# Half blocks of filler cut in two parts between scores and transposes, and the products of narrow attentions moved to VectorE ahead of the next maximum

## The chip, the cores and the metric

The kernel runs on one core of one Trainium2 chip. The metric is the time of one execution on the device, in microseconds; three runs of the kernel before gave 3421.99, 3423.82 and 3425.35 us, so the median is 3423.82 us. The profile is one more execution, recorded by the hardware profiler.

## The reference, cut to what matters

One sequence of 1024 tokens with 1024 features goes through three layers and two outer norms. All weights and activations are float32; the kernel splits each operand of a large product into a high and a low part and adds three products.

```python
# first_block, two layers: x = x + concat([mixed, mo]) @ w_out[l]; x = x + squared_relu_mlp(...)
#   layer 0: mixed = window_gqa (16 heads, 3 blocks of 128 keys, sink); layer 1: mixed = gated LRU
#   in both: mo = memory_attention(mq, mk, mv)
def memory_attention(mq, mk, mv):                      # 4 heads of 128, 256 memory tokens
    sc = einsum('bshd,bmhd->bhsm', mq, mk) * MEM_HEAD_DIM ** -0.5
    return einsum('bhsm,bmhd->bshd', softmax(sc, -1), mv)

# second_block, one layer on the output of the first, after its final norm
proj = h @ w_in                                        # h: modulated norm, 1024 x 3328
sb_q, sb_k, sb_v, sb_g, sw_q, sw_k, sw_v, sw_g = split(proj)
y_sb = stick_breaking_attention(sb_q, sb_k, sb_v) * silu(sb_g)      # 8 heads of 64
#   z = q k / 8; w = exp(log_sigmoid(z) + sum of log_sigmoid(-z) over the later keys), s < t
y_sw = sliding_window_sink_attention(sw_q, sw_k, sw_v) * silu(sw_g) # 8 heads, 256 keys, sink
x = x + gate * (concat([y_sb, y_sw]) @ w_out)
return rmsnorm(x, final_g)
```

## The kernel before, in words

Activations lie transposed, features on partitions and tokens on columns. A weight block is 128 x 1024: eight pieces of 128 x 128. `piece` and `split` (lines 228 to 249) load a block, copy it to its high part on ScalarE and subtract for the low part on VectorE, two blocks ahead of use; the load of a block three further on is issued on SP. A product of one block with 512 tokens is a "half chunk" (`half_chunk`, lines 351 to 371): 8 pieces x 3 = 24 matmuls of 512 columns into one PSUM bank, and a function `leave` that evacuates the bank. Half chunks are the filler of three kinds of stage.

All instructions are put in five queues in the order of the program text (class `Queues`, lines 40 to 111); each engine runs its own queue in order, and waits on the semaphores of an instruction's dependencies. So the order of calls is the schedule.

**Attention with units** (`attention_units`, lines 463 to 573). A unit is four heads (or, in the memory attentions, four blocks of queries) of 128 queries. It is used four times: with 384 keys ("full", 32 units of two groups of two, layer 0's window attention) and, narrow, with up to 256 keys, one group of four: the two memory attentions (8 units each) and the sliding-window attention of the last layer (16 units; units 0 and 1 have 128 keys). In step u the calls come in this order: `scores(u)`: matmuls on TensorE, the maximum of each row on VectorE (line 491), the negated maximum, with a sink also a sum for the sink, four exponentials on ScalarE with their sums, and the sink's exponential; `normalise(u-1)`: sum, reciprocal, and four products of a row's probabilities with its reciprocal, two on VectorE (line 515, recorded as line 148) and two on POOL (line 517); if `fills[u]` is 2, one filler call; `values(u-2)`: matmuls with V, and in every second unit the output block; the unit's side work if it has any; `turn(u-1)`: eight transposes on TensorE (line 526), which wait for the products; `copies(u-1)`: one bank copied by ScalarE, one by VectorE (line 539); and, if `fills[u]` is 1 or 2, one filler call.

In the memory attentions filler is the output projection (`half_chunks`), each call a whole half chunk with its evacuation. In the sliding-window attention filler is the gate's projection (`gate_chunk`, lines 1421 to 1426): eight half chunks in one bank, 7; each call first evacuates the half chunk before it (tanh on ScalarE, a product on VectorE). Two come before unit 0, the others in units 0, 1, 3, 5, 7 and 9. Output blocks (`out2`, line 1439) are a product on VectorE, a high copy on ScalarE and a subtraction on VectorE. Units 10 to 13 have side work: a row of 1024 columns is split into high and low (`to_parts`).

**Stick-breaking loop** (lines 1369 to 1405). 48 steps, each one block of 128 keys against up to 512 queries of two heads, pipelined over three steps. TensorE's order in step s is `pe_carry(s-3)`, `pe_within(s-2)`, `pe_scores(s)`, `pe_values(s-3)`, and in even steps up to 42 one half chunk (22 in all, in banks 6 and 7 in turn: gate, keys, queries). `pe_within` multiplies the high and the low part of a step's log terms, `sh` and `sl`, with a triangle. Behind TensorE's calls come those of ScalarE and VectorE: exponential, logarithm and combination `m` of step s-1, the copy of the scores of step s, the sum `add` of step s-2, `min` of step s, then `sh` on ScalarE and `sl` on VectorE of step s-1, and the last exponential of step s-2. A half chunk is evacuated at the end of the step behind it; a gate's evacuation is a tanh, with a table load before and one after it.

Of the kernel before, what the change touches and what calls it, by code (L numbers as in the profile page):

```python
# [13 lines left out]
KB = 1024  # L14
# [99 lines left out]
def program(nc, D, out, stop=None, dbg=None):  # L114
    ctx = ExitStack()
    with ctx:
# [234 lines left out]
        def half_chunk(name, bank, rhs, evac, hf, done):  # L351

            b = at[0]
            assert at[1] == 0
            piece(name)
            cs = slice(512 * hf, 512 * hf + 512)
            ps = PS[:, bank, :]
            for k in range(8):
                w = wsp[:, b % NS, :, k * 128:k * 128 + 128]
                rh, rl, ops = rhs(k)  # L360
                for i, (wi, r) in enumerate(((0, rh), (0, rl), (1, rh))):
                    op = mm(ps, w[:, wi, :], r[:, cs], k == 0 and i == 0, k == 7 and i == 2, splits[b], ops,
                            free[bank] if k == 0 and i == 0 else None)
            if done:
                uses[b] = [op]
                at[0] = b + 1

            def leave():
                free[bank] = [evac(cs, ps, op)]

            return op, leave

        def half_chunks(name, bank, rhs, evac):
            return [lambda n=n, hf=hf: half_chunk(name, bank, rhs, lambda cs, ps, op: evac(n, cs, ps, op), hf, hf == 1)[1]()
                    for n in range(8) for hf in range(2)]
# [87 lines left out]
        def attention_units(units, nkmax, off, scale, sink=None, fill=None, fills=()):  # L463
# [42 lines left out]
            def normalise(x):  # L506
                u, j, nk, sm_, es, rc, a = x
                if sink is not None:
                    a = TT(sm_, sm_, es, ALU.add, a)
                o = dve(lambda e: e.reciprocal(rc, sm_), a)  # L510
                last = [None, None]
                for i, pos in enumerate(groups[j]):
                    P_, r = Pb[:, u % 2, pos, 0:nk], rc[:, i:i + 1]
                    if i < w // 2:
                        last[0] = TS(P_, P_, r, None, ALU.mult, None, o)
                    else:
                        last[1] = pool(lambda e, P_=P_, r=r: e.tensor_scalar(P_, P_, r, None, ALU.mult), o)  # L517
                probs[J * u + j] = last
# [35 lines left out]
            for u in range(n + 2):  # L554
                for j in range(J):
                    x = scores(u, j) if u < n else None
# [3 lines left out]
                    if fill and fills[u] > 1:  # L560
                        fill.pop(0)()
# [8 lines left out]
                    if fill and fills[u] > 0:  # L570
                        fill.pop(0)()
# [734 lines left out]
        work = [lambda i=i, f=f, hf=hf: half_chunk("in2", 6 + i % 2, Hk, f(), hf, hf == 1)[1]  # L1306
# [62 lines left out]
        leave = None  # L1369
        for s in range(n_s + 3):  # L1370
# [8 lines left out]
            leaving, leave = leave, work.pop(0)() if s % 2 == 0 and work else None  # L1379
# [25 lines left out]
        assert not work and not leave  # L1405
# [13 lines left out]
        chunk, leave = [], []  # L1419

        def gate_chunk(t, hf):
            if leave:
                leave.pop()()
            op, late = half_chunk("in2", 7, Hk, fill_gate(WG, t, wg_done[t]), hf, True)
            chunk.append(op)
            leave.append(late)

        work = [lambda t=t, hf=hf: gate_chunk(t, hf) for hf in range(2) for t in range(4)]
        for _ in range(2):
# [19 lines left out]
        for k in range(4):  # L1449
            units[10 + k]["side"] = lambda k=k: to_parts(lambda _: SQ[:, k, :], lambda _: Hk(k), 1, chunk[7])  # L1450
        attention_units(units, 256, 80 * KB, 0.125, True, [*work[:2], lambda: leave.pop()(), *work[2:], lambda: leave.pop()()],
                        [1, 1, 1, 1, 0, 1, 0, 1, 0, 1, 1] + [0] * 7)
# [168 lines left out]
```

How the kernel before makes its waits and increments, by code:

```python
            def run(eng):  # L93
                seen = {}
                for o in self.q[name]:
                    for d in o.deps:
                        if seen.get(d.sem.name, 0) < d.val:
                            eng.wait_ge(d.sem, d.val)
                            seen[d.sem.name] = d.val
                    if o.fn is None:
                        continue
                    ins = o.fn(eng)
                    if o.sem is not None:
                        ins.then_inc(o.sem, 1 if o.sem is self.sems.get(name) else 16)
```

## Time and profile before

| | |
|---|---|
| median of 3 runs | 3423.82 us |
| profiled execution, its own time | 3419.25 us |
| its span, first to last instruction | 3417.5 us |
| granted TensorE clock, mean | 0.970 of full speed |
| TensorE busy | 3147.2 us, 92% |
| VectorE busy | 1689.4 us, 49% |
| ScalarE busy | 1112.8 us, 33% |
| POOL busy | 191.6 us, 6% |

Engines in the rows: PE is TensorE's matmuls, PEld its weight loads, DVE is VectorE, ACT is ScalarE, POOL is GpSimd, SP issues DMAs. "L283" is line 283, the helper `mm`, so matmuls are told apart by their operands: `PS<-H,wsp` is filler, `PS<-p,triR` the triangle products of the loop, L526 the transposes. Line 138 is the helper of ScalarE, 141, 144, 148 and 149 are those of VectorE. A row of a timeline is start, duration, engine, line, operation, output<-inputs, count; in brackets is the idle time of the engine ahead of it and who ended it. The stages of interest are the first memory attention (about 500 to 625 us), the second (1694 to 1830), the stick-breaking loop (2777 to 3122) and the sliding-window attention (3136 to 3312).

### The profile page before, as it was taken

How to read it: one execution, taken by the hardware profiler on the slowest of the kernel's cores; microseconds unless marked ns; L12 is line 12 of the kernel's file. 1: busy time of each engine (PE TensorE's matmuls, PEld its weight loads, DVE VectorE, ACT ScalarE, POOL GpSimd, SP SyncE). 2: the span in 40 equal slices, each digit the busy share in tenths (PEclk: the TensorE clock that was granted, in tenths of full speed). 3: DMA queues.
4: the chain of work that ended last, by engine and by line, in shares of the span. 5: the costliest groups of instructions: out<-in, count | busy, mean ns of one | idle time of the engine just before them, and what ended most of it. 6: DMA issues, size and time to landing. Idle time of an engine off the chain costs nothing.

```text
span 3417.5 us, 34713 instructions
## 1 busy us (share of the span) xinstructions
PE 3147.2 (92%) x14280; PEld 2419.9 (71%) x14298; DVE 1689.4 (49%) x2088; ACT 1112.8 (33%) x1729; POOL 191.6 (6%) x162
## 2 busy tenths in 40 slices
PE   4999989999999999999799999999997998997678
PEld 4777557778888888777677788888875775554456
DVE  6544864444444433589644433333336435554455
ACT  4202652311111111388523211111115336664332
POOL 0001431000000000000010000000003100000110
PEclk9999999999999999999999999999998999998889
DMA  4211011122222211211201111111111310002012
GB/s 163 99 38 32 1 55 33 37 74 73 69 74 69 73 50 54 76 47 47 99 31 44 43 50 50 44 50 48 45 49 56 117 37 19 19 19 74 19 50 99
DMA packets 54015, 190.19 MB, mean 56 GB/s; under 512 B 5984, under 2 KB 6368, under 8 KB 53728
## 3 DMA queue, kind: packets, MB, share of 16 engines
q1 hardware_dynamic: 53856, 187.96, 16.7%
q8 instruction: 113, 1.85, 0.2%
q14 instruction: 46, 0.38, 0.0%
HBM read 172.20 MB, written 14.68 MB: 55 GB/s over the span
## 4 chain that ended last, share of the span: by engine, by line
PE 76%; DVE 11%; ACT 9%; issue 2%; POOL 1%; DMA 0%; SPq 0%; DVEq 0%; ACTq 0%; POOLq 0%
PE PS L283 74%; ACT p L138 7%; DVE p L141 4%; PE PS L526 2%; DVE p L144 2%; DVE sm L491 2%; POOL p L517 1%; ACT H L138 1%; DVE p L1100 1%; ACT wsp L138 1%; DVE wsp L141 1%; DVE p L539 0%; ACT L138 0%; DVE p L149 0%; DVE sm L144 0%
## 5 line engine op out<-in xcount | busy, mean ns | idle before, releaser
L283 PE MATMUL PS<-H,wsp 128*128 128x512 f32 x6864 | 1617.8, 396 | 48.6 <-POOL H L1198 21.1
L283 PEld LDWEIGHTS PS<-H,wsp 128*128 128x128 f32 x6864 | 1299.8, 190 | 354.7 <-issue 28.4
L283 PE MATMUL PS<-p,wsp 128*128 128x512 f32 (+1 forms) x3840 | 896.2, 394 | 42.0 <-DVE p L141 21.5
L283 PEld LDWEIGHTS PS<-p,wsp 128*128 128x128 f32 x3840 | 714.3, 190 | 219.7 <-ACT wsp L138 37.7
L138 ACT ACTIVATE p<-p 128x1024 f32<-128x1024 f32 (+7 forms) x426 | 359.9, 871 | 852.0 <-DVE p L144 689.1
L138 ACT ACTIVATE wsp<-raw 128x1024 fp32r<-128x1024 f32 (+1 forms) x266 | 275.6, 1039 | 774.8 <-PE PS L283 632.6
L141 DVE TENSOR_TENSOR p<-p,PS 128x1024 f32<-128x1024 f32 (+2 forms) x232 | 244.3, 1053 | 526.4 <-PE PS L283 526.4
L141 DVE TENSOR_TENSOR wsp<-raw,wsp 128x1024 fp32r<-128x1024 f32 (+1 forms) x266 | 322.5, 1215 | 144.2 <-ACT wsp L138 144.1
L141 DVE TENSOR_TENSOR p<-PS,p 128x1024 f32<-128x1024 f32 (+1 forms) x124 | 143.0, 1153 | 442.6 <-PE PS L283 417.2
L283 PE MATMUL PS<-p 128*64 128x256 f32 (+9 forms) x1432 | 296.9, 480 | 15.0 <-DMA p<-mk_dram 5.0
L141 DVE TENSOR_TENSOR p<-p 128x1024 fp32r<-128x1024 f32 (+5 forms) x235 | 232.3, 991 | 112.1 <-ACT p L138 109.7
L517 POOL TENSOR_SCALAR p<-p,sm 128x256 f32<-128x256 f32 (+2 forms) x128 | 150.4, 1180 | 2297.2 <-DVE sm L510 2297.2
L138 ACT ACTIVATE p<-PS,sm 128x256 f32<-128x256 f32 (+2 forms) x256 | 127.9, 508 | 310.3 <-DVE sm L144 175.5
L144 DVE SCALAR_TENSOR_TENSOR p<-p 128x1024 f32<-128x1024 f32 (+3 forms) x167 | 189.3, 1141 | 68.4 <-ACT p L138 65.9
L138 ACT ACTIVATE p<-PS 128x512 f32<-128x512 f32 (+4 forms) x198 | 121.0, 638 | 264.1 <-PE PS L283 237.8
L283 PEld LDWEIGHTS PS<-p 128*64 128x64 f32 (+2 forms) x1432 | 127.5, 173 | 98.6 <-issue 60.5
L526 PE MATMUL PS<-cf,p 128*128 128x128 f32 x600 | 96.8, 300 | 79.6 <-POOL p L517 66.6
L526 PEld LDWEIGHTS PS<-cf,p 128*128 128x128 f32 x600 | 71.7, 152 | 115.5 <-issue 59.1
L491 DVE TENSOR_REDUCE sm<-PS 128x2 f32<-128x768 f32 (+3 forms) x96 | 94.9, 988 | 98.7 <-PE PS L283 98.2
L283 PE MATMUL PS<-p,triR 128*128 128x512 f32 (+3 forms) x352 | 86.5, 367 | 36.0 <-ACT p L138 19.8
L283 PEld LDWEIGHTS PS<-p,triR 128*128 128x128 f32 x352 | 56.5, 192 | 69.5 <-DVE p L141 34.3
L283 PE MATMUL PS<-wsp,H 128*128 128x256 f32 (+2 forms) x576 | 88.8, 316 | 0.0
(70 smaller groups left out, 1157.6 us busy)
## 6 DMA issues: line engine op xcount, KB each, us to landing
raw<-in_in_dram SPq DMA_DIRECT2D x70, 512.0 KB, 3.6
raw<-in_dn_dram SPq DMA_DIRECT2D x68, 512.0 KB, 3.5
raw<-in_up_dram SPq DMA_DIRECT2D x64, 512.0 KB, 3.5
raw<-in_out_dram SPq DMA_DIRECT2D x40, 512.0 KB, 3.6
p<-in_ada_dram SPq DMA_DIRECT2D x24, 512.0 KB, 4.5
raw<-in_kv_dram SPq DMA_DIRECT2D x16, 512.0 KB, 4.0
p<-in_x_dram SPq DMA_DIRECT2D x16, 512.0 KB, 8.7
spill_dram<-p SPq DMA_DIRECT2D x16, 512.0 KB, 2.9
```

The source lines that it names most:

```text
L138: return act(lambda e: e.activation(o, i, f, **kw), *a)
L141: return dve(lambda e: e.tensor_tensor(o, x, y, op), *a)
L144: return dve(lambda e: e.scalar_tensor_tensor(out=o, in0=x, scalar=s, in1=y, op0=op0, op1=op1), *a)
L283: return pe(lambda e: e.matmul(o, l, r, start=start, stop=stop, **kw), *a)
L491: o = dve(lambda e: e.tensor_reduce(mx, S, AX.X, ALU.max), op, prev)
L517: last[1] = pool(lambda e, P_=P_, r=r: e.tensor_scalar(P_, P_, r, None, ALU.mult), o)
L526: o = pe(lambda e, t_out=t_out, t_in=t_in: e.transpose(t_out, t_in, ident), probs[J * u + j], free[b])
L1100: L[("h", d)] = dve(lambda e: e.tensor_tensor_scan(out=dst, data0=da, data1=du, initial=0.0, op0=ALU.mult, op1=ALU.add), u, L[("a", d)], y ...
```

## The change: what it does

1. A half chunk is now a function `part(k0, k1)` that multiplies pieces k0 to k1 - 1, and `leave`. A whole one is `part(0, 8)`.
2. Loop: even steps up to 42 call `part(0, 4)`, the odd step behind each calls `part(4, 8)`; the evacuation comes at the end of the step behind that one, so one step later than before.
3. Sliding-window attention: each half chunk is two filler calls, `first` (evacuate the one before, 12 matmuls) and the rest (12 matmuls). Filler calls now all come between `scores(u)` and `values(u-2)`, none behind the transposes: two each in units 0, 1 and 2 (in unit 2: an evacuation alone, then a `first`), one each in units 3 to 10 (in unit 10 the last evacuation alone). So units 4, 6 and 8 begin a half chunk and units 3, 5, 7 and 9 end one.
4. Every narrow attention: all four products are on VectorE, and `normalise(u-1)` is called ahead of `scores(u)`, so it stands in VectorE's queue before the maximum of unit u.

The wide attention keeps its order and its products on POOL.

```diff
         def half_chunk(name, bank, rhs, evac, hf, done):
...
+            last = []
+
+            def part(k0, k1):
+                b = at[0]
+                assert at[1] == 0
+                piece(name)
+                for k in range(k0, k1):
...
+                last[:] = [op]
+                if done and k1 == 8:
+                    uses[b] = [op]
+                    at[0] = b + 1
 
             def leave():
-                free[bank] = [evac(cs, ps, op)]
-
-            return op, leave
+                free[bank] = [evac(cs, ps, last[0])]
+                return last[0]
+
+            return part, leave
...
-        def attention_units(units, nkmax, off, scale, sink=None, fill=None, fills=()):
+        def attention_units(units, nkmax, off, scale, sink=None, fill=None, fills=(), early=False):
...
-                    if i < w // 2:
+                    if i < w // 2 or not full:
                         last[0] = TS(P_, P_, r, None, ALU.mult, None, o)
                     else:
                         last[1] = pool(lambda e, P_=P_, r=r: e.tensor_scalar(P_, P_, r, None, ALU.mult), o)
...
                 for j in range(J):
+                    if pending and not full:
+                        normalise(pending)
+                        pending = None
                     x = scores(u, j) if u < n else None
                     if pending:
                         normalise(pending)
                     pending = x
-                    if fill and fills[u] > 1:
+                    for _ in range(fills[u] if fill and early else int(bool(fill) and fills[u] > 1)):
                         fill.pop(0)()
...
-                    if fill and fills[u] > 0:
+                    if fill and not early and fills[u] > 0:
                         fill.pop(0)()
...
-            leaving, leave = leave, work.pop(0)() if s % 2 == 0 and work else None
+            leaving = leave
+            leave = None
+            if s % 2 == 0 and work:
+                part, after = work.pop(0)()
+                part(0, 4)
+            elif s % 2 == 1 and after:
+                part(4, 8)
+                leave, after = after, None
...
+        def first(t, hf):
             if leave:
                 leave.pop()()
-            op, late = half_chunk("in2", 7, Hk, fill_gate(WG, t, wg_done[t]), hf, True)
-            chunk.append(op)
-            leave.append(late)
-
-        work = [lambda t=t, hf=hf: gate_chunk(t, hf) for hf in range(2) for t in range(4)]
-        for _ in range(2):
+            part, late = half_chunk("in2", 7, Hk, fill_gate(WG, t, wg_done[t]), hf, True)
+            part(0, 4)
+            leave.append(lambda: chunk.append(late()))
+            return part
+
+        for hf in range(2):
+            for t in range(4):
+                box = []
+                work.append(lambda t=t, hf=hf, box=box: box.append(first(t, hf)))
+                work.append(lambda box=box: box[0](4, 8))
+        for _ in range(4):
             work.pop(0)()
...
-        attention_units(units, 256, 80 * KB, 0.125, True, [*work[:2], lambda: leave.pop()(), *work[2:], lambda: leave.pop()()],
-                        [1, 1, 1, 1, 0, 1, 0, 1, 0, 1, 1] + [0] * 7)
+        attention_units(units, 256, 80 * KB, 0.125, True, [*work[:4], lambda: leave.pop()(), *work[4:], lambda: leave.pop()()],
+                        [2, 2, 2] + [1] * 8 + [0] * 7, True)
```

## Rows read from the trace of the kernel before

**Rows 1.** Stretches: length, then busy us (instructions) by engine, PEclk, DMA share, GB/s.

```profile
2788.60:3079.20 290.60, 263.00 (x1186) 165.80 (x1198) 161.82 (x203) 191.45 (x240) 0.00 (x0) 0.98 0.06 19
3150.18:3185.89 35.71, 24.35 (x110) 17.65 (x112) 12.62 (x28) 10.86 (x35) 4.45 (x6) 0.81 0.10 30
3185.89:3257.99 72.10, 48.89 (x242) 33.79 (x244) 29.41 (x61) 21.71 (x69) 11.91 (x12) 0.83 0.07 22
3257.99:3306.00 48.01, 27.85 (x165) 17.11 (x165) 30.24 (x63) 21.58 (x68) 13.90 (x14) 0.83 0.00 1
```

**Rows 2.** Waits of TensorE, 2788.64 to 3073.43: total us, times, longest.

```profile
PE PS L283 <- ACT p L138: 16.6, 19, 1.3
PE PS L283 <- DVE p L141: 8.5, 18, 1.1
```

**Rows 3.** Timeline of the loop, two steps of full width.

```profile
2933.44 5.74 PE L283 MATMUL PS<-H,wsp 128*128 128x512 f32 x24
...
2935.63 1.22 DVE L141 TENSOR_TENSOR p<-p 128x1024 fp32r<-128x1024 f32 x1 [0.25 <-ACT p L138]
...
2939.02 2.02 PE L283 MATMUL PS<-p,triR 128*128 128x512 f32 x8
...
2945.23 0.73 PE L283 MATMUL PS<-p,triR 128*128 128x512 f32 x2 [1.00 <-ACT p L138]
...
2946.49 0.73 PE L283 MATMUL PS<-p,triR 128*128 128x512 f32 x2 [0.53 <-DVE p L141]
```

**Rows 4.** Waits of all engines, 3122 to 3312.

```profile
PE PS L526 <- POOL p L517: 48.3, 16, 3.7
...
PE PS L283 <- DVE p L144: 12.3, 7, 3.8
```

**Rows 5.** Timeline of the loop behind a gate's evacuation.

```profile
2906.83 0.68 DVE L141 TENSOR_TENSOR p<-p 128x512 fp32r<-128x512 f32 x1
...
2908.49 1.08 PE L283 MATMUL PS<-p,triR 128*128 128x128 f32 x8
```

**Rows 6.** Timeline of the sliding-window attention, unit 7, and the maximum of unit 6.

```profile
3211.96 1.23 DVE L491 TENSOR_REDUCE sm<-PS 128x4 f32<-128x1024 f32 x1 [9.13 <-PE PS L283]
...
3218.80 1.22 DVE L491 TENSOR_REDUCE sm<-PS 128x4 f32<-128x1024 f32 x1 [0.92 <-PE PS L283]
...
3220.34 0.15 DVE L141 TENSOR_TENSOR sm<-sm 128x4 f32<-128x4 f32 x1
...
3220.74 0.84 DVE L148 TENSOR_SCALAR p<-p,sm 128x256 f32<-128x256 f32 x2
3220.80 1.99 POOL L517 TENSOR_SCALAR p<-p,sm 128x256 f32<-128x256 f32 x2 [4.85 <-DVE sm L510]
...
3222.21 0.63 ACT L138 ACTIVATE H<-p 128x512 fp32r<-128x512 f32 x1
...
3222.93 1.06 PE L526 MATMUL PS<-cf,p 128*128 128x128 f32 x8 [3.15 <-POOL p L517]
```

**Rows 7.** VectorE's groups by form, 2777 to 3312: busy us, mean ns | idle.

```profile
L539 DVE COPY p<-PS 128x512 f32<-128x512 f32 x14 | 9.7, 691 | 18.6 <-PE PS L526 18.5
...
L141 DVE TENSOR_TENSOR H<-p,H 128x1024 fp32r<-128x1024 f32 x4 | 4.9, 1226 | 3.9 <-ACT H L138 3.9
...
L149 DVE TENSOR_SCALAR p<-p 128x256 f32<-128x256 f32 x8 | 2.3, 285 | 0.0
```

**Rows 8.** Timeline of the sliding-window attention, unit 0.

```profile
3137.08 0.69 DVE L491 TENSOR_REDUCE sm<-PS 128x4 f32<-128x512 f32 x1 [5.34 <-PE PS L283]
...
3140.87 8.30 PE L283 MATMUL PS<-H,wsp 128*128 128x512 f32 x24 [3.83 <-DVE p L144]
```

**Rows 9.** Waits in the first memory attention, 500 to 622.

```profile
PE PS L526 <- POOL p L517: 5.4, 3, 2.1
```

**Rows 10.** Timeline of the second memory attention, unit 2.

```profile
1722.32 0.68 DVE L141 TENSOR_TENSOR p<-p,PS 128x512 f32<-128x512 f32 x1
...
1724.60 5.73 PE L283 MATMUL PS<-H,wsp 128*128 128x512 f32 x24
```

More of the change, by code:

```diff
@@ L351, in half_chunk, with whole @@
         def half_chunk(name, bank, rhs, evac, hf, done):
-            b = at[0]
-            assert at[1] == 0
-            piece(name)
             cs = slice(512 * hf, 512 * hf + 512)
             ps = PS[:, bank, :]
[L358 to L366, printed above, removed]
+            last = []
[4 more added lines that the diff above has]
+                for k in range(k0, k1):
+                    w = wsp[:, b % NS, :, k * 128:k * 128 + 128]
+                    rh, rl, ops = rhs(k)
+                    for i, (wi, r) in enumerate(((0, rh), (0, rl), (1, rh))):
+                        op = mm(ps, w[:, wi, :], r[:, cs], k == 0 and i == 0, k == 7 and i == 2, splits[b], ops,
+                                free[bank] if k == 0 and i == 0 else None)
+                last[:] = [op]
+                if done and k1 == 8:
+                    uses[b] = [op]
+                    at[0] = b + 1
             def leave():
-                free[bank] = [evac(cs, ps, op)]
-            return op, leave
+                free[bank] = [evac(cs, ps, last[0])]
+                return last[0]
+            return part, leave
         def half_chunks(name, bank, rhs, evac):
-            return [lambda n=n, hf=hf: half_chunk(name, bank, rhs, lambda cs, ps, op: evac(n, cs, ps, op), hf, hf == 1)[1]()
-                    for n in range(8) for hf in range(2)]
+            def whole(n, hf):
+                part, leave = half_chunk(name, bank, rhs, lambda cs, ps, op: evac(n, cs, ps, op), hf, hf == 1)
+                part(0, 8)
+                leave()
+            return [lambda n=n, hf=hf: whole(n, hf) for n in range(8) for hf in range(2)]
         Hops = [None] * 8
@@ L1305, in program @@
                 lambda: fill_keys(3), gate(3), *(lambda t=t: fill_query(t) for t in (1, 2, 3))]
[L1306 removed]
+        work = [lambda i=i, f=f, hf=hf: half_chunk("in2", 6 + i % 2, Hk, f(), hf, hf == 1)
                 for i, (f, hf) in enumerate((f, hf) for f in work for hf in range(2))]
@@ L1367, in pe_values @@
                     sg_free[pr] = o
-        leave = None
+        leave = after = None
         for s in range(n_s + 3):
@@ L1404, in program @@
                 leaving()
-        assert not work and not leave
+        assert not work and not leave and not after
         for par in range(2):
@@ L1418, in program @@
         wg_done = [[None, None] for _ in range(4)]
-        chunk, leave = [], []
-        def gate_chunk(t, hf):
+        chunk, work, leave = [], [], []
+        def first(t, hf):
             if leave:
                 leave.pop()()
-            op, late = half_chunk("in2", 7, Hk, fill_gate(WG, t, wg_done[t]), hf, True)
-            chunk.append(op)
-            leave.append(late)
-        work = [lambda t=t, hf=hf: gate_chunk(t, hf) for hf in range(2) for t in range(4)]
-        for _ in range(2):
+            part, late = half_chunk("in2", 7, Hk, fill_gate(WG, t, wg_done[t]), hf, True)
[8 more added lines that the diff above has]
+        for _ in range(4):
             work.pop(0)()
```

## The prediction

> **What bounds it now.** I read the busy shares of the page first (the table above): TensorE is busy for nearly all of the span and no other engine for half of it, so only TensorE's gaps, and the stretches in which its clock is halved, can be won. The table of stretches then says where the gaps are. The stick-breaking loop with filler, 2788.6 to 3079.2, has 290.6 us with 263.0 busy. The sliding-window attention, here from the maximum of unit 1 to the last transposes, is busy only some two thirds of the time, at a mean clock of 0.81 to 0.83 of full speed [rows 1]. The change touches nothing else, but for the two memory attentions; the loop's last steps have no filler and stay as they are.
>
> In the loop, the waits of TensorE are 16.6 us for ScalarE and 8.5 us for VectorE [rows 2]. The timeline of one pair of steps shows which: after the step with 24 filler matmuls (5.74 us) nothing is waited for, since VectorE's low part was done at 2935.63 + 1.22 = 2936.85, over 3 us before its reader. In the step without filler, TensorE waits 1.00 us for ScalarE's high part and 0.53 us for VectorE's low part [rows 3]. All filler covers one step, none the other.
>
> In the window attention two waits stand out: 48.3 us ahead of the transposes for POOL's normalisation, and 12.3 us for the bank of a filler chunk [rows 4].
>
> **Loop.** Removed: 24 matmuls in one place; added: 12 and 12. No instruction is added. Half of 5.74 is 2.87 us of cover for each step. In the step that had none, the waits 1.00 + 0.53 are under 2.87, so they go. The step that loses 2.87 us had a margin: 2939.02 plus half of 2.02 (the carries) plus two within matmuls, about 2940.5, against 2936.85, so 3.6 us. The tight place is behind a gate evacuation: low part ready at 2906.83 + 0.68 = 2907.5, wanted at about 2909.2 [rows 5], margin 1.7, which would leave 1.2 us of stall; but the evacuation now comes a step later. ScalarE and VectorE were busy 191 and 162 of 290 us [rows 1], so they can follow a loop some 25 us shorter. Evacuations, splits of weights and their loads on SP keep their order; a part's bank is the other one of two, free two steps on. Of the 25.1 us of waits, bounds are all gone and 10 gone; I take 21, leaving 4 around the eight gate evacuations. The clock of 0.98 is half speed for 4% of 290 us, which costs 5.8 us; fewer gaps may give back 0 to 5.8, I take 2. Loop: **-23 us** (-31 to -10).
>
> **Window attention, one unit at full width.** Now: maximum from 3218.80, exponentials and the sink's own until ScalarE is free at 3222.21 (3.4 us), POOL's two products 3220.80 to 3222.79, transposes 3222.93, 4.13 us behind the maximum [rows 6]. The unit's period, from maximum to maximum, is that plus 1.06 of transposes and some 1.7 of scores, 3218.80 - 3211.96 = 6.84 us [rows 6].
>
> With the change VectorE does all four products and has them ahead of the next maximum. That makes a ring on VectorE: maximum, wait for the exponentials (3.48 us from the maximum's start, the sink's included), sum and reciprocal (0.40, from 3220.34 to the first product [rows 6]), four products. The price of a product: 0.42 us in its present place beside POOL (two in 0.84, [rows 6]); 0.285 us for the nearest row without POOL, another constant-operand product of 256 columns [rows 7]. POOL will be idle, so I take 0.285 and keep 0.42 for the range. The Trainium skill ("SBUF — State Buffer", Terms) says that VectorE and GpSimd arbitrate for one port pair and the loser blocks for the other's whole instruction. By it a product without POOL would be cheap, as taken; without it, the sum below would be 6 us worse. With this rule the trace does not quite agree: both engines' products are recorded side by side [rows 6].
>
> Ring of a plain unit: 3.48 + 0.40 + 1.14 = 5.02 us. With an output block (every second unit) come ScalarE's copy 0.63 [rows 6], the bank copy 0.69 [rows 7] and a subtraction of the same width, taken to be as long, in order ahead of the next normalisation: 6.96. Units 10 to 13 also split a query row (1.23 on VectorE [rows 7], and a copy on ScalarE ahead of it, taken as 1.05): 7.9 to 8.45.
>
> Filler steps now come ahead of the transposes, but a chunk's first part evacuates the chunk before it, behind the unit's exponentials. The row of unit 0 shows that stall: 3140.87, which is 3.8 us behind the maximum at 3137.08 [rows 8]; with 256 columns the maximum is 0.5 longer and the exponentials 0.4: 4.8 us. So a pair of units from 4 on: 4.8 stall, part 2.87, values 1.0, transposes 1.0, bank copy 0.7, normalisation 1.54 = 11.95 for the first; the second, whose output block has to wait for the values behind its part, ends its normalisation 7.65 later: 19.6 us at full clock. Three such pairs now take 72.10 us [rows 1], 24.0 each. Of these 2 x 6.84 + 5.74 + 1.4 = 20.8 is the chain at full clock (1.4: the 12.3 us of bank waits [rows 4] less unit 0's 3.8, over six waits), and some 3 the halved clock. The stall with scores in front is a TensorE gap of 6.5 us, longer than today's 3.15; I add 2 us a pair for half clock behind it: 3 x 21.6 = 64.8, so -7.3.
> - Unit 1 to the maximum of unit 2: stall 3.8, a chunk as long as unit 0's 8.3 [rows 8], transposes 0.6, scores 1.7 = 14.4; units 2 and 3, a pair without output block in its first values: 19.9. Together 34.3 for 35.71 [rows 1]: -1.4.
> - Units 10 to 14: 8.45 + 8.45 + 7.93 + 8.45 + 5.02 = 38.3, unit 15 up to its transposes 7.1: 45.4 for 48.01 [rows 1]: -2.6.
>
> Window: -7.3 - 1.4 - 2.6 = **-11.3 us** (-18 to +5).
>
> **Memory attentions.** They keep their filler behind the transposes; only the normalisation moves. The first has 5.4 us of waits for POOL in three units [rows 9]; normalising during the scores saves all of two and half of the third: **-4.8** (-5.4 to -2). In the second, VectorE's queue also holds side work. Two normalisations of 1.35 us (without the sink's sum) now stand in front of maxima that start later, so ScalarE's split and the evacuation at 1722.32 come some 2.6 us later, past 1724.60, where the next chunk begins [rows 10]: **+1** (-2 to +3). The wide attention keeps its order and its POOL half: 0.
>
> **Sum.** -23 - 11.3 - 4.8 + 1 = -38.1 us. The profiled execution took 3419.25 us, which gives 3381.1; it lies 4.6 us under the median 3423.82, so **3386 us**.
>
> **Rivals.**
> - *The window attention gives nothing.* The stall for the bank is the long TensorE gap, and part, values and transposes behind it all run at half clock: a pair is 19.6 + 4.7, and with products at 0.42 another 1.1: 25.4, three are 76.2, 4 us slower than now; units 10 to 15 then cost 6 x 0.54 - 2.6 = +0.6, units 1 to 3 nothing. Window +5, total -22: 3402. For: the mean clock is already 0.83 there. Against: it is granted by stretches that need not meet the part. The Trainium skill ("TensorE: Matmul & The Clock Gate", HAM oscillation) has this rule, short bursts between waits keep the clock low; the trace agrees with it. Chance 0.21.
> - *The loop wins half.* The gate's activation and its two table loads on ScalarE meet steps whose cover is halved; eight stalls of 1.2 to 1.5 us stay: loop -12, total -27: 3397. Chance 0.15.
> - *Waits only move* from the bare step to the other, and the window is even: -5 or less: 3420. Chance 0.06.
> - *Slower.* Filler in the covered step was all needed: every even step then stalls 2.87 us, 22 x 2.87 = 63, less 25 won, +38 in the loop; with -15 elsewhere +23: 3447. It decides where the margin behind the 5.74 us is under some 1.2 us. The rows show 3.6 and 1.7. Chance 0.04.
>
> **Numbers.** The forecast has 0.54, its own range 3370 to 3395. A measurement of this kernel tells about 0.2%, 7 us, from no change. Faster by more: 0.54 + 0.21 + 0.15 = 0.90; within: 0.06; slower: 0.04. The range goes from all lower bounds (-31 - 18 - 5.4 - 2 = -56, 3367) to 6 us above the first rival, 3408; outside are the last two cases and thin tails.
>
> **What would show it.** In the loop, TensorE's waits for ScalarE and VectorE under 8 us in all, filler in groups of 12, the stretch some 268 us long. In the window attention no wait for POOL, products near 0.29 us, a wait of some 5 us for VectorE ahead of every second part, normalisations directly in front of maxima, and pairs of 20 to 22 us. Products at 0.42 us, pairs over 24 us or loop waits still above 15 us would prove the corresponding step wrong; a loop longer than 290 us would overthrow the forecast.

## The result and the profile after

The changed kernel takes 3371.86 us (median of four executions, 3369.49 to 3372.85) against 3422.90 us for the kernel before (four executions, 3418.16 to 3425.35): a ratio of 0.9852, 95% interval 0.9834 to 0.9869. That is 51 us faster, where 38 were forecast, and inside the predicted range of 3367 to 3408 us. The profiled execution took 3372.85 us, its span is 3371.1 us, 46.4 less than before's 3417.5.

The table divides both spans at the same instructions. Idle is the length less TensorE's busy time; "half clock" is the time, in us, in which TensorE was granted the lower of its two clocks.

| stretch | before, us | after, us | difference | half clock, before and after |
|---|---|---|---|---|
| up to the first memory attention | 500.0 | 503.5 | +3.5 | |
| first memory attention | 132.6 | 125.5 | -7.1 | 3.4, 0 |
| second memory attention | 140.9 | 143.1 | +2.2 | 18.7, 18.5 |
| loop, first scores to the gate's filler | 346.0 | 311.5 | -34.5 | 23.9, 6.8 |
| filler ahead of the window's first maximum | 13.9 | 15.5 | +1.6 | 0, 3.4 |
| window, first maximum to output projection | 175.0 | 159.4 | -15.6 | 64.9, 65.7 |
| behind it | 105.3 | 108.2 | +2.9 | 8.2, 16.0 |

The rest, in which the program is the same, differs by under 1 us.

**The loop.** These are the stretches of the profile of after: the loop's steps with filler, its steps without, then in the window units 1 to 3, 4 to 9, and 10 to 15 as far as the last transposes. Columns as in [rows 1].

```profile
2776.47:3051.80 275.33, 269.25 (x1262) 171.76 (x1263) 164.92 (x211) 202.45 (x252) 0.00 (x0) 0.99 0.07 22
3051.80:3088.00 36.20, 25.16 (x92) 10.82 (x92) 22.66 (x22) 24.05 (x25) 0.00 (x0) 0.95 0.00 1
3116.19:3150.32 34.13, 24.00 (x108) 17.19 (x108) 13.74 (x34) 10.82 (x35) 0.00 (x0) 0.80 0.09 31
3150.32:3213.48 63.16, 45.55 (x248) 31.54 (x248) 30.85 (x73) 21.57 (x69) 0.00 (x0) 0.84 0.08 26
3213.48:3257.57 44.09, 31.01 (x156) 17.26 (x157) 30.61 (x72) 20.88 (x68) 0.00 (x0) 0.74 0.00 1
```

The same two parts of the loop in the kernel before:

```profile
2777.15:3079.20 302.05, 273.78 (x1229) 173.22 (x1244) 164.43 (x208) 197.54 (x248) 0.00 (x0) 0.98 0.06 20
3079.20:3123.18 43.98, 31.64 (x110) 13.19 (x111) 25.07 (x25) 26.91 (x28) 0.00 (x0) 0.88 0.00 1
```

The filler now reaches one step further, so the two rows are best added. Idle time: 346.0 - 305.4 = 40.6 before, 311.5 - 294.4 = 17.1 after, so 23.5 us less. Busy time: 305.4 before, 294.4 after, 11.0 us less for the same matmuls, and that is what the forecast had at 2. The trace of before lacks 16 of the loop's 1352 matmul records, so a little of its busy time is counted as idle. The kernels e2 and e3 below have the loop undivided and all 1352 records: 38.6 us idle, 306.2 us busy, 20.5 us at half clock. Against them the division takes away 21.5 us of idle time and 11.8 of busy time. Waits of TensorE in after, in the part with filler, in the form of [rows 2]:

```profile
PE PS L283 <- DVE p L141: 5.6, 9, 1.4
PE PS L283 <- DVE p L911: 2.7, 1, 2.7
```

Against [rows 2], ScalarE's waits are gone, and of VectorE's half are left by count and two thirds by length (the one of line 911 stands ahead of the loop's first step, in before too). Two steps of the widest kind in after, where every 12 matmuls of filler stand ahead of eight triangle products, none of which waits:

```profile
2925.37 2.02 PE L283 MATMUL PS<-p,triR 128*128 128x512 f32 x8
...
2928.97 3.02 PE L283 MATMUL PS<-H,wsp 128*128 128x512 f32 x12
...
2931.24 1.22 DVE L141 TENSOR_TENSOR p<-p 128x1024 fp32r<-128x1024 f32 x1
2931.82 2.02 PE L283 MATMUL PS<-p,triR 128*128 128x512 f32 x8
```

Eight triangle products take 2.02 us; in [rows 3] the last four of the bare step came two at a time, each pair with a wait ahead of it and 0.73 us long instead of 0.50. By these records, whose ends are modelled, a wait costs its length and about 0.2 us more. The other part of the 11 us is the clock: half clock fell from 23.9 to 6.8 us, and 17.1 us at the lower level are worth at most half, 8.5. How the 11 us divide between the two was not measured.

**The window attention.** TensorE's largest waits in after, from the last filler ahead of it to the output projection, against [rows 4]:

```profile
PE PS L283 <- DVE p L144: 31.1, 6, 6.2
PE PS L283 <- ACT p L138: 8.0, 6, 2.6
PE PS L534 <- DVE p L148: 3.7, 6, 0.8
```

POOL's 48.3 us are gone. The wait for the filler's bank (line 144 is the evacuation's product) has grown from 12.3 to 31.1 us, six times about 5 us instead of seven times about 1.8. The timeline of after from the products of unit 7 to the maximum of unit 9, against [rows 6]:

```profile
3191.68 1.14 DVE L148 TENSOR_SCALAR p<-p,sm 128x256 f32<-128x256 f32 x4
3192.73 1.22 DVE L499 TENSOR_REDUCE sm<-PS 128x4 f32<-128x1024 f32 x1
...
3196.09 0.60 ACT L138 ACTIVATE p<-PS 128x512 f32<-128x512 f32 x1
...
3196.73 0.69 DVE L144 SCALAR_TENSOR_TENSOR p<-p,PS 128x512 f32<-128x512 f32 x1 [2.38 <-ACT p L138]
...
3197.47 4.48 PE L283 MATMUL PS<-H,wsp 128*128 128x512 f32 x12 [6.21 <-DVE p L144]
...
3205.36 3.01 PE L283 MATMUL PS<-H,wsp 128*128 128x512 f32 x12
3206.10 1.22 DVE L499 TENSOR_REDUCE sm<-PS 128x4 f32<-128x1024 f32 x1
```

The products stand directly ahead of the maximum, four in 1.14 us. The tanh of the evacuation (3196.09) comes behind the unit's four exponentials, so the bank is free 4.7 us behind the maximum of unit 8; TensorE has been idle for 6.2 us by then, and the first part runs partly at half clock, 4.48 us for what takes 3.01 in the second. A pair of units is 13.4 to 14.0 plus 7.4 us.

**The memory attentions.** TensorE's wait for the products in the first one, in after, against [rows 9]:

```profile
PE PS L534 <- DVE p L148: 0.3, 1, 0.3
```

Unit 2 of the second one, timeline of after, against [rows 10]:

```profile
1720.94 0.68 DVE L141 TENSOR_TENSOR p<-p,PS 128x512 f32<-128x512 f32 x1
...
1721.68 4.61 PE L283 MATMUL PS<-H,wsp 128*128 128x512 f32 x12 [3.35 <-DVE p L141]
```

The 5.4 us for POOL became 0.3. In the second, the chunk now waits 3.35 us for the bank that the evacuation at 1720.94 frees. The line counts only the 12 matmuls up to the end of the view, at 1726; the whole chunk of 24 took 7.37 us, with 3.4 us of it at half clock, against 5.73 in [rows 10].

### The profile page after: what moved, and what is told of

Same layout as the page of the kernel before. It is cut to its first block, busy times and chain, and to the rows that moved or that the text cites. A ratio compares the mean times of both kernels' runs of the same rounds, so it can differ in the third digit from the quotient of the medians.

```text
span 3371.1 us, 34684 instructions
## 1 busy us (share of the span) xinstructions
PE 3144.4 (93%) x14298; PEld 2421.0 (72%) x14298; DVE 1695.2 (50%) x2152; ACT 1113.1 (33%) x1729; POOL 128.8 (4%) x98
## 3 DMA queue, kind: packets, MB, share of 16 engines
q1 hardware_dynamic: 53856, 187.96, 17.1%
## 4 chain that ended last, share of the span: by engine, by line
PE 74%; DVE 12%; ACT 11%; issue 2%; POOL 1%; DMA 0%; SPq 0%; DVEq 0%; ACTq 0%; POOLq 0%
PE PS L283 73%; ACT p L138 8%; DVE p L141 4%; DVE p L144 2%; DVE sm L499 1%; PE PS L534 1%; ACT H L138 1%; ACT wsp L138 1%; DVE p L1111 1%; DVE p L148 1%; DVE H L141 1%; DVE wsp L141 1%; ACT L138 1%; DVE p L547 0%; DVE p L149 0%
## 5 line engine op out<-in xcount | busy, mean ns | idle before, releaser
L283 PE MATMUL PS<-p,wsp 128*128 128x512 f32 (+1 forms) x3840 | 897.3, 394 | 42.1 <-DVE p L141 21.6
L283 PE MATMUL PS<-p 128*64 128x256 f32 (+9 forms) x1432 | 290.7, 470 | 23.3 <-ACT p L138 10.7
L525 POOL TENSOR_SCALAR p<-p,sm 128x384 f32<-128x384 f32 (+1 forms) x64 | 87.7, 1370 | 411.5 <-DVE sm L518 411.5
L415 POOL TENSOR_TENSOR p<-p 128x512 f32<-128x512 f32 x14 | 20.6, 1471 | 2095.9 <-DVE p L415 2065.7
L283 PE MATMUL PS<-p,triR 128*128 128x512 f32 (+3 forms) x352 | 78.9, 357 | 15.3 <-DVE p L141 14.6
```

The source lines that it names most:

```text
L283: return pe(lambda e: e.matmul(o, l, r, start=start, stop=stop, **kw), *a)
L415: lambda e: e.tensor_tensor(self.acc, self.acc, sq, ALU.add), a, self.op)
```

## The experiments

Each is compared with the kernel before on the same chip; the chips differ between groups of experiments, so across them the ratios count and not the medians. In the table, window and loop are lengths in the profiled execution, between the instructions of the table above; "units 4-9" is the stretch of three pairs.

| kernel | median, us | ratio to before, interval | loop | window (half clock) | units 4-9 | units 10-14 |
|---|---|---|---|---|---|---|
| before | | | 346.0 | 175.0 (64.9) | 72.1 | 39.6 |
| after | 3371.86 | 0.9852 [0.9834, 0.9869] | 311.5 | 159.4 (65.7) | 63.2 | 37.3 |
| e1_loop | 3389.15 | 0.9907 [0.9885, 0.9930] | 312.1 | 170.5 (55.6) | 71.9 | 35.8 |
| e2_window_parts | 3402.22 | 0.9952 [0.9934, 0.9971] | 344.8 | 155.0 (38.6) | 61.7 | 34.2 |
| e3_normalise | 3396.10 | 0.9935 [0.9911, 0.9959] | 344.8 | 154.5 (58.6) | 61.3 | 37.2 |
| e6_parts_7_1 | 3385.47 | 0.9899 [0.9875, 0.9923] | 325.8 | 159.2 (62.2) | 63.2 | 37.2 |
| e4_pool_ahead | 3372.39 | 0.9864 [0.9842, 0.9886] | 312.1 | 160.5 (62.8) | 63.0 | 36.6 |
| e5_vector_behind | 3368.47 | 0.9852 [0.9832, 0.9871] | 311.9 | 154.4 (54.6) | 61.8 | 34.5 |
| e7_evac_first | 3337.35 | 0.9760 [0.9742, 0.9779] | 312.1 | 125.2 (24.5) | 45.3 | 36.8 |
| e8_evac_first_behind | 3330.60 | 0.9738 [0.9716, 0.9759] | 312.1 | 119.9 (23.9) | 41.5 | 37.3 |
| e9_whole_filler | 3366.65 | 0.9860 [0.9844, 0.9877] | 311.5 | 155.9 (65.4) | 61.2 | 37.2 |
| e10_products_as_before | 3371.78 | 0.9871 [0.9857, 0.9886] | 311.9 | 157.1 (45.4) | 61.9 | 34.2 |
| e11_mixed | 3325.19 | 0.9738 [0.9723, 0.9752] | 311.8 | 117.3 (13.7) | 41.5 | 35.9 |

**The three parts of the change, each alone.** e1_loop keeps the loop's part and takes the other two back. Against the kernel before, beside the new `half_chunk`:

```diff
+            if s % 2 == 0 and work:
+                part, after = work.pop(0)()
+                part(0, 4)
+            elif s % 2 == 1 and after:
+                part(4, 8)
+                leave, after = after, None
```

> Only the loop's half chunks are cut in two; the attentions are as before. Theory (the gain is cover for the bare step: 22 us of waits, about 8 us of half clock that the waits had brought about, and some 4 us of restarts of TensorE's stream): -30 to -36 us against before, about 3389, loop waits for ScalarE and VectorE under 8 us in the part with filler, half clock in the loop under 12 us. Rival (the part that is not waits is a chance of the clock's timing): -20 to -25 us, half clock in the loop again over 18 us.

The loop is 33.9 us shorter, its half clock is 6.8 us as in after, and the ratio is 0.9907, 32 us. So the -34.5 of after belong to this part alone, and they are no accident of one execution: the loop takes 311.5 to 312.1 us in all nine kernels of the table that divide the filler as the change does, and 344.8 in the two that don't divide it, 346.0 in the kernel before. The change also evacuates each half chunk one step later, and no run has one of the two without the other.

e2_window_parts keeps only the window's filler parts; the products stay as before:

```diff
-        attention_units(units, 256, 80 * KB, 0.125, True, [*work[:2], lambda: leave.pop()(), *work[2:], lambda: leave.pop()()],
-                        [1, 1, 1, 1, 0, 1, 0, 1, 0, 1, 1] + [0] * 7)
+        attention_units(units, 256, 80 * KB, 0.125, True, [*work[:4], lambda: leave.pop()(), *work[4:], lambda: leave.pop()()],
+                        [2, 2, 2] + [1] * 8 + [0] * 7, True)
```

> Only the filler of the sliding-window attention is cut and moved ahead of the transposes; products are on VectorE and POOL behind the maximum as before, the loop is as before. Theory (filler ahead of the transposes hides POOL's products, and there is no ring on VectorE): pairs of units from 4 on 18 to 21 us instead of 24, units 10 to 15 as before at 48 us, window -11 to -15 us in all, POOL waits left only in units 10 to 15 (some 18 us). Rival (the wait for the bank takes the place of the wait for POOL): window within 3 us of before.

e3_normalise keeps only the products:

```diff
-                    if i < w // 2:
+                    if i < w // 2 or not full:
...
+                    if pending and not full:
+                        normalise(pending)
+                        pending = None
```

> Only the products of narrow attentions are on VectorE ahead of the next maximum; filler is whole and behind the transposes, the loop is as before. Theory: no waits for POOL; in the window, pairs from 4 on 20 to 22 us, units 10 to 15 44 to 46 us, together -9 to -13 us; first memory attention -5 to -7, second +2: -14 to -18 us in all. That and the window's parts alone would then overlap: their sum is more than the 15.6 us that both have together. Rival (parts and products add up): window -2 to -4 us here.

Both gave more than expected in the window: 20.0 us for the filler parts, 20.5 for the products. In the total, by the ratios, that is 16 us for e2 and 22 for e3, the latter above the 14 to 18 expected. Together, in after, they give 15.6 in the window. The ratios say the same without any single profile: e1, e2 and e3 alone gain 32, 16 and 22 us, 70 in sum, and the whole change 51. The window of e1, with the program of before, took 170.5 us, so all three window gains would be 4.5 smaller against it, but their order stays. TensorE's waits in the window of e2_window_parts:

```profile
PE PS L283 <- DVE p L144: 28.3, 7, 4.9
PE PS L534 <- POOL p L525: 21.9, 10, 3.2
```

And in the window of e3_normalise:

```profile
PE PS L283 <- DVE p L144: 23.3, 6, 4.7
PE PS L283 <- ACT p L138: 10.5, 8, 2.9
PE PS L534 <- DVE p L148: 5.8, 6, 2.0
```

Either edit takes most of the wait for the products (48.3 to 21.9, or to 5.8), and in either the bank of the filler comes to the front, with 28.3 and 23.3 us. The second edit has only the rest of the same wait to take, and other waits take that back. Against e3 the loss lies in units 0 to 9, where the bank's wait grew to 31.1 us: the earlier TensorE is through with the unit before, the longer it stands at the bank. Against e2 the larger part of it, 3.1 us, lies in units 10 to 14, which have no filler: with the products ahead of the maximum a unit there takes 7.7 to 8.2 us in after, and 6.8 in e2. In the pairs of units 4 to 9 the two kernels with one edit took 61.7 and 61.3 us, after 63.2.

Of e2's 20.0 us, 5.4 lie in units 10 to 14, which have no filler and, but for the place of the last evacuation, the same program as before; they took 34.2 us instead of 39.6. In e2_window_parts, units 10 to 15 up to the transposes were at full clock:

```profile
3244.18:3286.77 42.59, 21.66 (x165) 13.36 (x165) 30.11 (x63) 21.34 (x68) 13.88 (x14) 1.00 0.00 1
```

Against the 0.83 in the last line of [rows 1] TensorE needs 21.7 us in place of 27.9 for these matmuls. e10_products_as_before, whose window has the same program as e2's, shows 34.2 again; but e1_loop, whose window has the program of before, shows 35.8 for before's 39.6, with 3.4 us at half clock for 13.7. So 3.8 of the 5.4 differ between two executions of one program. The other 1.6 are unit 10 alone, 8.4 us and partly at half clock in before and e1, 6.8 and at full clock in e2 and e10; they may come with the edit, whose filler ahead of that unit is placed otherwise.

**Does cover count by its length?** In the loop the rival was that any filler in the bare step would do. e6_parts_7_1 puts 21 matmuls into the even step and 3 into the odd one:

```diff
-                part(0, 4)
+                part(0, 7)
             elif s % 2 == 1 and after:
-                part(4, 8)
+                part(7, 8)
```

> The changed kernel, but the loop's half chunks are cut into 21 and 3 matmuls instead of 12 and 12. Theory (cover counts by its length): the bare step has 0.72 us of cover, so some 0.8 us of waits a pair stay, 12 to 20 us in all, and some half clock comes back: 10 to 20 us slower than the changed kernel, 3382 to 3392. Rival (what counts is that the step has any filler, or that the evacuation comes a step later): within 4 us of the changed kernel.

The loop is 325.8 us, 14.2 longer than after's; 9.1 of that is idle time, 5.1 busy. TensorE's waits in the whole loop of e6_parts_7_1:

```profile
PE PS L283 <- DVE p L141: 19.3, 26, 2.4
PE PS L283 <- ACT p L138: 5.6, 10, 1.4
```

One of its odd steps in the timeline, TensorE alone:

```profile
2930.84 0.96 PE L283 MATMUL PS<-H,wsp 128*128 128x512 f32 x3
2931.64 1.10 PE L283 MATMUL PS<-p,triR 128*128 128x512 f32 x4
2933.04 0.73 PE L283 MATMUL PS<-p,triR 128*128 128x512 f32 x2 [0.30 <-ACT p L138]
2934.30 0.73 PE L283 MATMUL PS<-p,triR 128*128 128x512 f32 x2 [0.53 <-DVE p L141]
```

With 0.7 us more of cover, the wait for ScalarE shrank from 1.00 to 0.30 and the one for VectorE behind it stayed at 0.53 [rows 3]: each low part comes a fixed time behind its high part, so cover that is too short for both leaves the second wait whole. So cover counts by its length. The numbers also leave little for the later evacuation, which e6 has too: ScalarE's waits in the loop are 21.4 us in e2 and 5.6 here, 15.8 less, and 22 steps with 0.7 us of cover are 15.4.

**Are the products on VectorE needed, and is their place?** e4_pool_ahead gives POOL its half back, ahead of the maximum:

```diff
-                    if i < w // 2 or not full:
+                    if i < w // 2:
```

> The changed kernel, but in narrow attentions two of the four products go back to POOL, still ahead of the next maximum. Theory (the cycle maximum, exponentials, sum, products on VectorE sets the unit; POOL's half is off it): products shorten from four to two beside POOL, units within 0.5 us of the changed kernel, window 156 to 162 us, total within 5 us of the changed kernel. Rival (taking POOL off the way to the transposes was what gained): window 8 us or more longer.

e5_vector_behind leaves all four on VectorE, but behind the maximum, as before the change:

```diff
-                    if pending and not full:
-                        normalise(pending)
-                        pending = None
```

> The changed kernel, but the products, all on VectorE, come behind the next maximum as before the change. Theory (being ahead of the maximum closes a cycle on VectorE, and costs where filler hides the products anyway): pairs of units from 4 on 18 to 20 us instead of 21, units 10 to 14 31 to 34 us instead of 37.3, window 145 to 152 us; first memory attention 3 us longer, second 2 us shorter; total 5 to 12 us faster than the changed kernel, 3360 to 3367. Rival (ahead of the maximum is what wins): window longer than 160 us, total slower than the changed kernel.

Both take as long as after within their intervals. For e4, POOL's products ahead of the maximum are hidden in units 4 to 9, where TensorE waits for the bank alone. In units 10 to 15 its transposes wait six times, 10.2 us in all, against 3.7 us in after. The profile puts 8.5 of these to VectorE's negated maximum, but each time the transposes start 0.14 to 0.15 us behind the end of POOL's products, as in [rows 6]; so it is POOL that they wait for. Units 10 to 14 took 36.6 us all the same, after's 37.3. For e5, the window is 5 us shorter than after's, the second memory attention 3.2 us shorter (139.9), the first 4.2 us longer (129.7, of which up to 1.7 is 3.4 us of half clock). The forecasts for its window, 145 to 152 us, and for its total, at most 3367 us, were below what came, 154.4 and 3368.47; the bank's wait is still there, 28.3 us.

**Is the bank what bounds the window now?** e7_evac_first moves the evacuation of a half chunk from in front of the next one to the end of the unit in which the half chunk was completed, behind the transposes and the bank copies:

```diff
-            if leave:
+            if leave and t + 4 * hf == 1:
                 leave.pop()()
...
+        leave.pop()()
...
+                    if u in tail:
+                        tail[u]()
...
-        attention_units(units, 256, 80 * KB, 0.125, True, [*work[:4], lambda: leave.pop()(), *work[4:], lambda: leave.pop()()],
-                        [2, 2, 2] + [1] * 8 + [0] * 7, True)
+        attention_units(units, 256, 80 * KB, 0.125, True, work,
+                        [2, 2] + [1] * 8 + [0] * 8, True, {u: lambda: leave.pop()() for u in (0, 1, 3, 5, 7, 9)})
```

The call of `leave` by itself evacuates the second half chunk ahead of unit 0.

> The changed kernel, but a gate chunk is evacuated at the end of the unit that finishes it, ahead of the next unit's exponentials, and not in the middle of the next unit. Theory (a chunk's first part waits 5 to 6 us for the bank because the evacuation is queued behind four exponentials): these waits go, pairs from 4 on 15 to 17 us, unit 0 and 1 3 to 4 us shorter each; window 135 to 145 us, total 15 to 24 us faster, 3348 to 3357. Rival (TensorE then waits as long for the products): window over 154 us.

e8_evac_first_behind is the same with e5's edit.

> Both edits together: evacuation at the end of the unit that finishes the chunk, and the products on VectorE behind the maximum. Theory: no cycle through VectorE and no wait for the bank; pairs from 4 on 13 to 15.5 us, near TensorE's own work, units 10 to 14 31 to 34 us; window 124 to 136 us, total 24 to 35 us faster than the changed kernel, 3337 to 3348, below both kernels. Rival (the two edits cover the same wait): no faster than the better of the two alone.

By their medians e7 is 34.5 us under after and e8 41.3; by the ratios, 0.9760 and 0.9738 against 0.9852 with intervals that don't touch, it is 31 and 39. Both are better than expected, in the window (125.2 and 119.9 us) and in the total. The window's stretch in e7_evac_first:

```profile
3102.55:3227.73 125.18, 101.11 (x564) 66.74 (x565) 79.47 (x191) 56.63 (x185) 0.00 (x0) 0.90 0.11 35
```

The same stretch in after:

```profile
3103.47:3262.90 159.43, 112.34 (x565) 74.58 (x565) 81.33 (x191) 57.58 (x186) 0.00 (x0) 0.79 0.09 28
```

TensorE's wait for the bank in that stretch of e7_evac_first:

```profile
PE PS L283 <- DVE p L144: 6.8, 5, 2.2
```

And its timeline where an evacuation stands in its new place:

```profile
3159.85 1.09 ACT L138 ACTIVATE p<-PS 128x512 f32<-128x512 f32 x2
...
3161.21 0.68 DVE L144 SCALAR_TENSOR_TENSOR p<-p,PS 128x512 f32<-128x512 f32 x1
...
3161.94 4.37 PE L283 MATMUL PS<-H,wsp 128*128 128x512 f32 x11 [1.86 <-DVE p L144]
```

The tanh is now called with the bank copy at 3159.85, ahead of the next unit's exponentials, and TensorE waits 1.86 us instead of 6.21. The part behind this short wait was still partly at half clock, 4.37 us for the 11 matmuls that the view holds and 4.61 for all 12; two units earlier, behind the same wait, it took 3.03. Of the 34.2 us between the two stretches, 11.2 are busy time of the same matmuls (112.3 to 101.1, with half clock down from 65.7 to 24.5 us) and 23.0 idle, about what the bank's wait lost (31.1 to 6.8).

**Each window edit taken out of after.** e9_whole_filler puts the whole half chunks back behind the transposes, e10_products_as_before takes both of e4's and e5's edits:

```diff
-                work.append(lambda t=t, hf=hf, box=box: box.append(first(t, hf)))
-                work.append(lambda box=box: box[0](4, 8))
-        for _ in range(4):
+                work.append(lambda t=t, hf=hf: (first(t, hf)(4, 8), chunk.append(Q.last("pe"))))
+        for _ in range(2):
             work.pop(0)()
...
-                        [2, 2, 2] + [1] * 8 + [0] * 7, True)
+                        [1, 1, 1, 1, 0, 1, 0, 1, 0, 1, 1] + [0] * 7)
```

> The changed kernel with the window's filler whole and behind the transposes again (loop cut, products on VectorE ahead of the maximum). Theory (filler ahead of the transposes and products ahead of the maximum cover the same wait, and together they only add the wait for the bank in mid-unit): window 150 to 158 us against 159.4, total 0 to 9 us faster than the changed kernel. Rival (each part of the change adds its own gain): window over 165 us, slower than the changed kernel by 6 us or more.

> The changed kernel with the products on VectorE and POOL behind the maximum as before (loop cut, window's filler cut and ahead of the transposes). Theory: window 150 to 160 us; first memory attention 5 to 7 us longer than in the changed kernel, second 2 us shorter: total within 6 us of the changed kernel. Rival (the products bring their own gain): slower by over 10 us.

Neither can be told from after: 0.9860 and 0.9871 against 0.9852, with intervals that overlap, and windows of 155.9 and 157.1 us. Either edit can be left out at no cost that these runs can tell, as long as the other stays; they are two covers for one wait.

**The best of both.** e11_mixed is e8 with the products ahead of the maximum in the first memory attention alone, where e5 had shown a loss:

```diff
-                    if pending and not full:
+                    if pending and ahead:
...
-            attention_units(units, 256, off, 128 ** -0.5, fill=fill, fills=fills)
+            attention_units(units, 256, off, 128 ** -0.5, fill=fill, fills=fills, ahead=not side)
```

> The fastest kernel so far (gate chunk evacuated at the end of its unit, products on VectorE behind the maximum), but in the first memory attention the products come ahead of the maximum. Theory (ahead pays where the filler is behind the transposes and no side work is queued): first memory attention 125 to 128 us instead of 129.7, all else the same, total 2 to 5 us below the 3330.6 us of that kernel. Rival: no difference that can be told.

3325.19 us, the lowest median of the study, but on a chip where the kernel before is 4 us faster as well; its ratio equals e8's, so the last edit's share in the time is not shown. In the profiles its stage behaves as expected: the first memory attention takes 127.2 us, with 129.7 in e8 and the same 3.4 us at half clock in both, and e7 and e8, which differ in the same edit, show 127.2 and 129.7 too. Either kernel is about 1.2% faster than the changed one (0.9738 / 0.9852).

## Why the prediction was right or wrong

The direction and the order of size were right, -38 against -51, and every step but one gave more than its forecast; stretches that the change does not touch gave a part of it back.

| step | forecast | bounds | measured | with the edit alone |
|---|---|---|---|---|
| loop | -23 | -31 to -10 | -34.5 | -33.9 (e1) |
| window, units 4 to 9 | -7.3 | | -8.9 | |
| window, units 1 to 3 | -1.4 | | -1.6 | |
| window, units 10 to 15 | -2.6 | | -3.9 | |
| window, whole | -11.3 | -18 to +5 | -15.6 | -20.0 (e2), -20.5 (e3) |
| first memory attention | -4.8 | -5.4 to -2 | -7.1 | |
| second memory attention | +1 | -2 to +3 | +2.2 | |

The window's remaining 1.2 us lie in unit 0 and behind the last transposes. The measured steps sum to -55.0; the stretches outside them gave back 8.6 us in this pair of executions (the start, the filler ahead of the window, and the end, whose half clock was 16.0 us for 8.2), which makes the span's -46.4. The medians differ by 51 because before's profiled execution, 3419.25, lay under its median and after's, 3372.85, above.

- **Loop: the mechanism held, a term was too small.** The forecast took 21 of the 25.1 us of waits, and 2 of the clock: idle time fell by 23.5 (21.5 against e2 and e3, whose records are complete), and the busy time by 11.0 (11.8) where 2 was taken. The wait was sized rightly, the busy time was not. Two things were not priced: that a matmul behind a wait is longer (0.73 for 0.50, to be read in [rows 3] itself), and that nearly all of the half clock would go. The bound of -31 was thus no bound. "The loop's last steps have no filler and stay as they are" was wrong too: the filler reaches one step further. The rival "the loop wins half" is refuted by e1; the rival "slower", filler all needed in the covered step, by VectorE's waits of 5.6 us in the part with filler, and e6 shows what the choice of 12 and 12 is worth, 14 us.
- **Window: the stall was forecast, and nearly to the tenth.** Forecast 4.8 us behind the maximum with a gap of 6.5, measured 4.7 and 6.2; product 0.285 us, measured 1.14 for four; plain ring 5.02, measured 5.13; pair 21.6, measured 20.8 to 21.4; units 10 to 13 8.45 and 7.93, measured 8.2 and 7.7. Of the 4.3 us beyond the forecast, 3.1 are small margins over 15 units; 1.2 lie where nothing was forecast. Two of the prediction's sums are off by less than 0.1 us, the first unit of a pair (its terms add up to 11.91, not 11.95) and the ring with an output block (7.03, not 6.96), and how 7.9 to 8.45 is reached isn't said.
- **The rival "the window gives nothing"** had its condition right and its extent wrong: the part behind the stall did run at half clock, for 4.48 us instead of 3.02, but the values and transposes behind it at full clock (1.08 and 1.09 us), and the second part too. The Trainium skill ("TensorE: Matmul & The Clock Gate", HAM oscillation) describes a kernel whose bursts of matmuls are shorter than the waits between them, so that each burst starts at the low clock; the runs agree in direction: the window's half clock is 65.7 us with the bank's waits at 31.1 and 24.5 us with them at 6.8. It did not eat the gain. The bank is not alone in it: e2 had 38.6 us at half clock with 28.3 us of the same waits.
- **What the prediction missed in the window** is that it priced the two edits as one. It had the stall for the bank at its right size, but asked neither whether one of the edits would lead to the same stall, nor what moving the evacuation would be worth (34 us of the window, e7, more than either). The size of the window's gain also depends on which execution stands for the old program: against e1's window, 170.5 us, after's gain is 11.1 and not 15.6.
- **First memory attention:** the three waits of 5.4 us went whole where half of the third was to stay. Of the 7.1, 1.7 is that before's execution had 3.4 us of half clock there and after's none: e2, with the products as before and no half clock, took 130.9, and against that after's 125.5 is -5.4.
- **Second memory attention:** held. The evacuation came late for the next chunk's bank, as forecast, by 3.35 us once; the wait for the products ahead of the first transposes shrank from 11.6 to 9.3 us.
- **Price of a product.** The forecast took 0.285 us with POOL idle and kept 0.42. By the rule that VectorE and GpSimd block each other (the Trainium skill, "SBUF — State Buffer", Terms), taking POOL out had to help. These are VectorE's and POOL's products in e4_pool_ahead, in the window (line, operation, count, then busy us, mean ns of one, idle us):

```profile
L148 DVE TENSOR_SCALAR p<-p,sm 128x256 f32<-128x256 f32 x28 | 11.7, 461 | 0.5
...
L525 POOL TENSOR_SCALAR p<-p,sm 128x256 f32<-128x256 f32 x28 | 27.7, 1000 | 106.7 <-DVE sm L518 106.7
```

And in e5_vector_behind, without:

```profile
L148 DVE TENSOR_SCALAR p<-p,sm 128x256 f32<-128x256 f32 x56 | 16.0, 350 | 0.5
```

Busy time by count, since the records of one engine overlap, one costs 0.42 us beside POOL (11.7 / 28) and 0.285 alone (16.0 / 56), so the trace agrees that they disturb each other, though not that one stands still for the other's whole instruction (1.0 us on POOL). In time it made nothing: e4 and after cannot be told apart.

## What to carry to other kernels

Where work can cover waits in several steps, ask how long the cover of each step must be, and give each that much: 24 matmuls in one of two steps left TensorE 38.6 us idle in the loop (e2, e3), 21 and 3 left 26.3, 12 and 12 17.1. Count the price of a wait with what follows it, the slower restart and the half clock; here that was half as much again as the waits. Before two edits are added that attack the same wait, price each alone, and ask of the pair which wait comes next: here it was a bank whose evacuation was called behind four exponentials, and moving that one call was worth twice what both edits had won in that stage.

## What the runs showed of the hardware that was not expected

- One stretch of one program, units 10 to 14, took 39.6 us in before and 35.8 in e1, with 13.7 and 3.4 us at half clock. In e2, nearly the same program, it took 34.2 us with none; with unit 15 the mean was 0.83 of full speed in before and 1.00 in e2.
- Removing 23.5 us of idle time from the loop removed 17.1 of its 23.9 us at half clock; against e2 and e3 it was 21.5 us of idle time and 13.7 of 20.5.
- A part of 12 filler matmuls takes 3.01 us at full clock. In units 4, 6 and 8 of after, behind gaps of 6.21 us, it took 5.15, 4.72 and 4.48; behind gaps of 1.86 us in e7 3.03 and 4.61; behind gaps of 0.75 us in e8 3.01, 3.06 and 3.01.
- Two 512-column matmuls behind a wait of 0.3 to 1.0 us take 0.73 us, the same two in a row of eight 0.50, by records whose ends are modelled.
